# The mixers' instructions merged in another order on four engines

## The reference

```python
h = rmsnorm(x, W['norm_mix'][i])
cp = h @ W['w_in'][i]
ca, cb, cc = ...                       # columns of the three groups
ya, sh, Sa = rwkv7_mixer(ca, ...)      # 6 heads: token shift, decay, delta-rule recurrence
yb, Sb = retention_mixer(cb, ...)      # 4 heads
yc, cv, hc = mamba2_mixer(cc, ...)     # 6 heads: convolution over 4 tokens, SSD recurrence
x = x + jnp.concatenate([ya, yb, yc], axis=-1) @ W['w_out'][i]
h = rmsnorm(x, W['norm_ffn'][i])
x = x + swiglu(h, ...)                 # layer 0; layer 1: moe_swiglu
```

## Time and profile before

| | us |
|---|---|
| median of 3 runs | 1403.95 (1399.22 to 1405.0) |
| profiled execution, its own time | 1401.54 |
| its span in the trace | 1399.7 |
| PE busy in the span | 1326.7 (95%) |
| DVE, ACT, POOL busy | 938.2, 720.0, 136.0 |

### The profile page before, as it was taken

One profiled execution on the slowest core, in us unless ns is written; L12 is line 12 of the kernel. 1 busy time (PEld: TensorE's weight loads), 2 busy tenths in 40 slices (PEclk: granted clock), 3 DMA queues, 4 the chain that ended last, 5 costly groups with the idle time before them and its releaser, 6 DMA issues.

```text
span 1399.7 us, 26188 instructions
## 1 busy us (share of the span) xinstructions
PE 1326.7 (95%) x10133; PEld 1156.3 (83%) x10133; DVE 938.2 (67%) x1492; ACT 720.0 (51%) x1097; POOL 136.0 (10%) x160
## 2 busy tenths in 40 slices
PE   5999999989999999899999998989999999999996
PEld 4899887768999999889988876877787787778775
DVE  5485755445655556748676453559888897898887
ACT  5633454114433343363335421467778777777774
POOL 1031310030000000002121002000100100100011
PEclk9999998559999999899999865999999999999997
DMA  6321320035444444133122002639879897897982
GB/s 251 117 93 33 107 99 16 12 108 213 149 151 164 151 151 151 39 109 108 48 92 98 32 12 76 231 120 337 311 263 330 309 338 254 317 335 260 351 302 81
DMA packets 62919, 235.05 MB, mean 168 GB/s; under 512 B 7264, under 2 KB 7488, under 8 KB 62048
## 3 DMA queue, kind: packets, MB, share of 16 engines
q1 hardware_dynamic: 59760, 217.61, 44.5%
q0 software_dynamic: 2336, 12.81, 2.4%
q10 hardware_dynamic: 720, 3.18, 0.6%
HBM read 225.48 MB, written 8.09 MB: 167 GB/s over the span
## 4 chain that ended last, share of the span: by engine, by line
issue 33%; PE 19%; ACT 2%; DVE 2%; POOL 1%; POOLq 0%; DVEq 0%; ACTq 0%
PE bank L562 4%; PE bank L568 3%; PE bank L570 2%; PE bank L569 2%; PE bank L1049 1%; POOL x L2686 1%; PE bank L722 1%; PE bank L733 1%; PE bank L729 1%; ACT whi L1323 0%; PE bank L937 0%; PE bank L589 0%; PE bank L798 0%; PE bank L984 0%; PE bank L950 0%
## 5 line engine op out<-in xcount | busy, mean ns | idle before, releaser
L1323 ACT ACTIVATE whi<-wraw 128x1024 fp32r<-128x1024 f32 x410 | 433.0, 1060 | 395.9 <-PE bank L570 309.8
L1795 DVE TENSOR_TENSOR wlo<-wraw,whi 128x1024 fp32r<-128x1024 f32 x410 | 500.8, 1227 | 201.1 <-ACT whi L1323 196.5
L568 PE MATMUL bank<-hh,whi 128*128 128x320 f32 x608 | 202.2, 333 | 16.6 <-DVE wlo L1795 4.7
L569 PE MATMUL bank<-hl,whi 128*128 128x320 f32 x608 | 191.8, 315 | 0.0
L570 PE MATMUL bank<-hh,wlo 128*128 128x320 f32 x608 | 191.7, 315 | 0.0
L1242 PE MATMUL bank<-whi,hh 128*128 128x512 f32 (+1 forms) x384 | 147.3, 384 | 3.7 <-DVE wlo L1795 3.2
L1244 PE MATMUL bank<-wlo,hh 128*128 128x512 f32 (+1 forms) x384 | 143.4, 373 | 0.0
L1243 PE MATMUL bank<-whi,hl 128*128 128x512 f32 (+1 forms) x384 | 143.0, 373 | 0.0
L568 PEld LDWEIGHTS bank<-hh,whi 128*128 128x128 f32 x608 | 117.6, 193 | 29.6 <-issue 11.0
L569 PEld LDWEIGHTS bank<-hl,whi 128*128 128x128 f32 x608 | 118.5, 195 | 0.0
L570 PEld LDWEIGHTS bank<-hh,wlo 128*128 128x128 f32 x608 | 117.8, 194 | 0.0
(11 more groups left out here) (411 smaller groups left out, 2285.0 us busy)
## 6 DMA issues: line engine op xcount, KB each, us to landing
wraw<-in_w SPq DMA_DIRECT2D x410, 512.0 KB, 5.0
smb<-in_s_ssm POOLq DMA_DIRECT2D x2, 1536.0 KB, 7.7
out_o_ssm<-smb POOLq DMA_DIRECT2D x2, 1536.0 KB, 12.0
cst<-in_consts ACTq DMA_DIRECT2D x1, 2161.0 KB, 12.9
srw<-in_s_rwkv POOLq DMA_DIRECT2D x2, 768.0 KB, 4.8
out_o_rwkv<-srw POOLq DMA_DIRECT2D x2, 768.0 KB, 3.6
x<-in_x SPq DMA_DIRECT2D x1, 1280.0 KB, 5.7
out_y<-x SPq DMA_DIRECT2D x4, 320.0 KB, 2.2
```

The source lines that it names most:

```text
L568: mm(out, hi, rh, start=first, stop=False)
L569: mm(out, hi, rl, start=False, stop=False)
L1323: af(whi[:, ring % HI, :], wraw[:, POS[ring], :], ACT.Copy).then_inc(S("slot_hi"), 1)
L1795: tt(wlo[:, POS[ring], :], wraw[:, POS[ring], :], whi[:, ring % HI, :].bitcast(F32), ALU.subtract).then_inc(S("slot_split"), 1)
```

## The change

The four lists of names are replaced by others of the same length with the same names the same number of times. No instruction is added or taken away but loads of activation tables, which go by neighbours on ACT. In PE's list, the first inversion step stood behind 26 steps of `in` of 60, and now stands behind 41. The last step of `in` stood at place 135 of 197, and now at place 132. Two lines of it:

```diff
@@ PE_TURNS (the whole list is new; 8 lines) @@
-    in in in in in in in in prep in in in in in in prep in in in in in in prep in in in in in in inv2 inv1 in
+    in in in in in in prep in in in in in in in prep in in in in in in in in in in in in in in in in in in in
 ...
@@ DVE_TURNS, ACT_TURNS, POOL_TURNS: new as well @@
```

More of the change, by code:

```diff
@@ L155 @@
-    rw0 mb1 rw0 rw0 cb1 rw0 mb1 cb1 cb1 rw0 cb1 tok1 mb2 tok1 tok1 rw0 rt0 rt0 rw1 mb2 rt0 rw1 mb2 rt1 rw1 rw1
-    rt1 mb2 rt1 rw1 rt1 rt1 rw1 rt1 mb2 rt1 rw1 rw1 rt2 rw1 rt2 rw1 rt2 rw1 rt2 rt2 rt2 late late rt2 late late
-    late late late late
+    in in in in in in prep in in in in in in in prep in in in in in in in in in in in in in in in in in in in in
+    in in in in prep in in in in inv2 in inv1 inv0 inv2 inv1 inv2 inv0 prep inv0 inv2 prep in inv2 in inv2 sS in
+    in cb2 cb2 inv0 in in sS sS in sS in dt cb2 cb2 inv0 in in tok2 dt tok2 inv1 in in inv1 tok2 inv0 inv1 inv0
@@ L158 @@
+    inv1 inv0 inv1 inv0 inv1 inv0 inv1 inv0 in in rw2 in rw2 inv1 rw2 inv1 nS rw2 inv1 inv0 rw2 cb0 cb0 nS cb0
+    cb0 rt0 rw2 tok0 nS rt0 in mb0 tok0 tok0 rt0 in mb0 rt0 mb0 rw0 in rw0 mb0 rw0 rw0 rw0 mb0 rw0 rt0 rt0 rw0
+    rt0 rw0 cb1 rw0 cb1 cb1 rw0 tok1 rw0 cb1 rt1 tok1 tok1 mb1 rt1 rw1 rt1 mb1 rw1 rt1 rt1 mb1 rw1 rt1 rw1 mb1
+    rw1 mb1 rw1 rt1 mb2 rt2 rw1 rw1 rt2 mb2 rw1 mb2 rt2 rw1 mb2 rw1 mb2 rt2 rt2 rt2 late late rt2 late late late
+    late late late
 """
 ACT_TURNS = """
-    dt in in in in prep prep in in in in prep prep prep in in in in prep in in prep prep in in in in in in in in
@@ L161 @@
[L161 to L164, removed]
+    dt in in prep in in in in prep prep prep prep in in in in prep in in prep prep in in in in in in in in in in
@@ L165 @@
+    in in in in in in in in in in conv in in conv in conv in conv in in in in conv in in conv prep conv prep
+    prep in in in in in in sS in in dt dt in tok2 in dt tok2 in in tok2 in rw2 rw2 rw2 tok0 in mb0 tok0 rt0 tok0
+    mb0 mb0 rt0 rt0 in rw0 rw2 mb0 mb0 rt0 rw0 mb0 rt0 rw0 rw0 rw0 tok1 rw0 tok1 tok1 mb1 mb1 rt1 mb1 rw1 rt1
+    rt1 rt1 mb1 mb1 rw1 mb1 rt1 mb2 mb2 rw1 mb2 rw1 rt2 rw1 mb2 mb2 mb2 rw1 rt2 rt2 rt2 rt2
 """
 DVE_TURNS = """
-    prep in in in in in in in prep in in in in in in prep in in in in prep in prep prep in prep prep in in inv2
@@ L168 @@
[L168 to L176, removed]
+    prep in in in in in in prep in in in in in prep in in in in in in in in in in in in in in in conv conv conv
+    conv in conv conv conv conv in conv conv conv conv in conv conv conv conv prep prep prep prep prep prep conv
@@ new lines @@
+    conv inv2 conv conv conv inv2 conv inv2 inv1 inv1 inv0 inv1 inv0 inv2 inv2 inv0 conv inv2 inv0 conv inv0
+    conv conv conv conv inv0 in in inv2 in inv1 inv1 inv2 inv2 in cb2 cb2 in inv0 in dt cb2 cb2 in inv0 dt dt dt
+    dt dt dt dt dt dt dt in dt inv1 dt in in in in inv1 inv0 inv1 inv0 inv1 inv0 inv1 inv0 inv1 inv0 inv1 inv0
+    rw2 xs inv1 rw2 inv1 xs nS inv1 inv0 nS cb0 cb0 rw2 xs nS cb0 nS rt0 rw2 rt0 rw2 rt0 rw2 nS rt0 nS cb0 mb0
+    mb0 mb0 mb0 rw0 mb0 mb0 rw2 mb0 rw0 mb0 rw0 rw0 rt0 mb0 mb0 rt0 rw0 rt0 rw0 rt0 mb0 rt0 cb1 cb1 cb1 rw0 rw0
@@ L177 @@
+    cb1 rw0 rw0 rt1 rw0 rt1 rt1 rt1 mb1 rw1 mb1 rt1 mb1 mb1 rw1 rw1 rt1 mb1 mb1 mb1 mb1 rw1 mb1 mb1 rt1 mb1 rt1
+    rt1 rt2 rt2 rw1 mb2 rt2 rt2 mb2 mb2 mb2 rw1 mb2 mb2 mb2 mb2 rw1 mb2 rw1 rw1 mb2 rw1 rt2 rt2 rt2 late late
+    rt2 rt2 rt2 late late late late late late
 """
 POOL_TURNS = """
-    prep prep shift conv conv prep conv conv conv conv xv conv conv xv xv xv xv mb0 rt0 mb1 mb2 rt1 rt1 conv mb1
-    rt2 rt2 mb2 rt2 mb2
+    prep shift conv conv conv conv prep conv conv conv conv prep xv xv xv rt0 xv mb0 xv rt1 mb1 rt1 conv mb1 rt2
@@ L181 @@
+    mb2 rt2 mb2 rt2 mb2
 """
```

## The result

The changed kernel takes 1434.31 us (median of 4 runs, 1433.88 to 1436.2), the kernel before 1401.59 us (1397.14 to 1405.0) beside it: a ratio of 1.0238, 95% interval 1.0203 to 1.0273. Slower was forecast, but by 14 us; it is 33 us.

The account below looks back on a forecast made before the run. PE, busy 1326.7 of 1399.7 us, was taken as the bound, so only its waits and clock could change. Terms of 1.9+1.1+4.4+1.3+1.5+0-3=7.2 us per layer, 14.4 in both, gave 1418 us; 8-in-10 range 1396 to 1440.

Parts of the forecast that it names:

- The first block of ACT: Small projections' sigmoids: a table load and tile sigmoid now directly before them lengthen PE's wait by 1.9 us per layer.
- The second table block: A slot later, ACT's table load, square root and scalings precede slot 9's high part: 1.1 us per layer, 0 to 2.
- The start of the inversions: PE waits for the preparation and `Wm` behind DVE's `brx`, convolutions and masks: 4.4 us per layer, from 1 to 7.
- The bare inversions: 12 inversion steps without filling, and the five steps before them, make PE wait 1.3 us per layer, 0 to 4.
- The chains' waits: Tail of the mixers: waits for Mamba's norm, retention's sum and the last norm change by 0, from -2 to +3.
- The clock behind a wait: The inversions' 2.6 us wait adds one half-clock dip, 1.5 us per layer; the first block keeps its own.
- Where the clock falls for good: End of the mixers: 8-column products some 22 us later may delay the clock's fall; 3 us won per layer.
- the sign that I had set: Wrong in the clock if low stretches are more than 15 us longer or shorter than before's 78 and 60 us.
- The sentence from the Trainium skill: A VectorE copy of a result doesn't end TensorE's warm state; by it the 1.5 us dip would fall away.
- The one on shared ports: VectorE and GpSimd block each other in SBUF: six convolutions beside POOL's product cost some 1 us more per layer.
- the clock falls early: Rival: clock falls within the last inversions or at the last projection step; 1440 us as a mean, chance 0.17.

Follow-up runs that it names:

- tail_new: The kernel before up to about 216 us of a layer, then the changed kernel's order for the chunk chains; 1418.54 us.
- inv_old: The changed kernel with everything up to about 84 us of a layer taken from the kernel before; 1411.82 us.
- after_spread: The changed kernel with projection steps held back and spread on PE, its other PE order kept, the other engines' lists fitted to it; 1405.53 us.
- fill12: The kernel before with nine added PE steps of 12 unused matmuls per layer among the chunk chains; 1408.93 us.
- tail_swap: tail_new with one pair of steps exchanged on ACT, so the copy `SA` stands before retention's root; 1413.99 us.
- spread_undone: few_waits_spread with its last eight projection steps 1 to 10 us earlier, PE's other order kept, other engines' lists refitted; 1390.92 us.
- few_waits_spread: The kernel before with single steps moved on all engines for few PE waits, with a price on long stretches without projection steps; 1389.71 us.
- merged: A further search from few_waits_spread with a higher price on stretches without a projection step; 1411.63 us.
- front_new: The kernel before with only the changed kernel's first pieces, up to PE's second step of `prep`; 1407.24 us.

## Why the prediction was wrong

**The first block of ACT** was right: 1.9 us forecast, 1.87 measured (4.04 less 2.17). The second table block gave 0.68 us at 63 us instead of 1.1.

**The start of the inversions** was right in size, 4.4 forecast and 3.8 to 4.1 measured, but not in its parts: the preparation itself, which I gave 0.5 us, cost 2.03; `Wm` cost 1.96 instead of 2.6, and the next one 0.1 to 0.4 instead of 1.2. PE got to the place earlier relative to DVE than I had added up.

**The bare inversions** cost less in waits than I said (0.2 us instead of 0.6; PE's 12 steps stand nearly gapless), and the wait ahead of them for the chain of 18-column DVE instructions behind a low part (`d_dA`) was 0.8 us, where I had 0.7: 1.0 of 1.3 us in sum. The chains' waits came out at 6.0 us, where the kernel before has 5.0 to 6.4: nothing, as forecast.

Together the waits were to be 8.7 us per layer (1.9, 1.1, 4.4, 1.3 and 0) and are 6.8 and 9.0. If it had been only for them, the forecast would stand.

**The clock behind a wait** was too small. The dip at the start of the inversions cost some 3 us (an estimate: 6.8 us at half clock in both layers), twice the 1.5; that of the first block grew from 3.4 to 6.8 us, which cost 0.5 to 1 us more, and I had let it stay; the wait of 1.0 us at 26 us, which is in both kernels, brought a dip of 1.6 us in layer 0 here and none before, and that of 1.27 us ahead of 944 us one of some 3 us. I had read one dip in the earlier trace rows and priced the second by it. The waits of the kernel before that had no dip behind them were there to be seen, and they would have told that a wait of the same length may cost nothing or twice itself.

**Where the clock falls for good** is the step that failed: "Mamba's 8-column products, which now stand some 22 us later" were to hold the fall back, 3 us won per layer. The clock fell at 227 us in layer 0 and 807 us in layer 1, 63 us ahead of these products, with no wait of PE in the 19 us before it. The low stretches at the ends of the mixers grew by 3.3 and 6.8 us, which by the ratio 1.71 of the earlier trace rows is a loss of some 1.4 and 2.8 us (an estimate) instead of 3 us won in each. tail_new, with these products late and nothing new before 216 us, fell at 221 us. I had made a trigger out of one place in layer 1; and there the clock had not held: it was low for 3.4 us from 793 us and 6.8 us from 800 us, which I passed over as a break. Nor did it fall for good: in both layers of the changed kernel it came back for some 14 us in the midst of the chains. By the sign that I had set, 15 us more or less than 78 and 60 us, layer 0 is unchanged and layer 1, with 78 us, is over it only because my 60 left out those two. These two steps are the 18 us between forecast and result: some 10 us from the sign of the last in both layers, and the rest, some 9 us, from the dips, the 3 us at 944 us among them, while the waits were over-counted by 1.6.

The sentence from the Trainium skill that I weighed (TensorE: Matmul & The Clock Gate, "Loop structure matters more than you think") speaks of a copy by VectorE behind which the next matmuls follow immediately. Here PE stood idle for 4.04 us, and the 7 us from 47 us on show 0.58; so the rows don't contradict the sentence, but my conclusion from it, that the dips would fall away, was wrong. The one on shared ports (SBUF — State Buffer, "Who interferes with whom") would have added 1 us per layer. DVE's six convolution instructions at the start of the inversions took 0.45 to 0.58 us each, without any such loss, but POOL's product of the preparation had run from 105.35 to 108.69 us, before the first of them at 113.43: my placing of the two beside each other was wrong, and this trace does not test the sentence.

Of the rivals, "the clock falls early" had the price nearest (1440 us, chance 0.17), but its sum was wrong: 7.2+3+12 to 18 is 22 to 28 us per layer, or 1448 to 1460 us, which is hardly nearer than the forecast. Its mechanism is half of it: the clock did fall 7 us behind the last projection step, but not for good, and the bare inversions ran at 1.00. inv_old and after_spread put two thirds and more of the loss on what stands before and at the start of the inversions, where PE had spent its filling.

What stays open is what exactly lets the clock fall. Shown is: added filling puts it off (fill12), and the order of the chains brings it on 10 to 12 us sooner in layer 0 (tail_new and tail_swap), also without the wait of 1.4 us. That taking filling from the inversions brings it on there rests on one trace (spread_undone) whose other engines' lists differ as well; against it, the 14 us of inversions without any filling in the changed kernel ran at 1.00. Waits have their part, by their place more than by their length. In the fifteen traces a wait of 0.9 to 1.1 us for Mamba's norm found the clock at full twenty times, and nineteen times it fell within 3 us; the wait of 2.0 us for `Wm` (L715) was followed by a dip five times out of five, and the wait of 1.35 us for `htk_l` (L1183) in layer 1's feed-forward part not once in fifteen. But the fall at 227 us in the changed kernel stands behind 19 us without a wait, and so does the one at 807 us in layer 1. Not explained are 38 us of chains at full clock with no filling (few_waits_spread, layer 0), and that the same lists fall at other places in layer 1 than in layer 0 and from run to run.

## What to carry to other kernels

Reordering a kernel whose TensorE is at 95% can win or lose on two accounts, waits and clock, and the waits can be added up from the trace beforehand to a few us; the clock can't, and here it was half of the loss. When work that runs without waiting (filling) is limited, spread it over the stretches that depend on other engines rather than spend it ahead of them: in after_spread it hid 14.6 of 33.9 us of waits and won 29 us. But merged, made with a higher price on stretches without filling than few_waits_spread, was 22 us slower than that, so every such merge has to be measured. Judge a low-clock event by all its likes, in every trace at hand and those where nothing happened too, before pricing the next; and look at single runs, since such kernels spread over 20 us with nothing changed.

Two of the experiments beat both kernels, few_waits_spread (ratio to before 0.993, 0.9898 to 0.9963) and spread_undone (0.9918, 0.9891 to 0.9945).

## What the runs showed of the hardware

The clock explains the time between runs of one kernel: front_new's runs with a mean granted clock of 0.925 and 0.940 have spans of 1414.8 and 1399.5 us, 1 us for each 0.001. A dip behind a wait of 1.0 to 4.0 us lasts 3 to 7 us and costs 1.5 to 3 us, when it comes: 3.4 us long at 26 us behind a wait of 1.0 us, 6.8 us behind waits of 1.27, 2.0 and 4.04 us. Whether it comes hangs on the place: behind the 1.27 us ahead of the feed-forward's `hidh` in 14 of 15 traces, behind the 1.35 us for `htk_l` in none. A long stretch of low clock can end while the chains go on: at 0.50 from 227 to 251 us, at 0.99 from 254 to 267 us, with the last projection step at 220 us. It need not: in front_new it stayed at 0.50 from 237 to 322 us.
